# The last gated embedding and the final norm, turned so that tokens lie in the partitions

## What is computed

```python
def rmsnorm(x, g):
    y = x * lax.rsqrt(jnp.mean(x * x, axis=-1, keepdims=True) + 1e-6)
    return y * g

# end of the last layer (i = 1), h is [256, 1024], p[i] is [256, 256]
gate = jax.nn.sigmoid(rmsnorm(h, ple_norm[i]) @ ple_gate[i])   # ple_gate[i]: [1024, 1024]
h = h + (p[i] @ ple_proj[i]) * gate                            # ple_proj[i]: [256, 1024]
return rmsnorm(h, final_norm)
```

## Time and profile before

| | us |
|---|---|
| median of 3 runs (lowest, highest) | 1065.03 (1064.36, 1066.72) |
| the profiled execution's own time | 1066.18 |
| its span | 1064.4 |
| PE busy in the span | 1047.7 |
| DVE busy | 770.6 |
| ACT busy | 609.4 |
| first gate matmul of the last embedding starts | 1030.02 |
| its last gate matmul starts | 1054.12 |
| first of the four stores is issued | 1059.36 |

### The profile page before, as it was taken

How to read it: one execution, slowest core, us unless ns; L and a number is a source line. 1 busy time by engine, 2 the same in 40 slices (tenths; PEclk the granted TensorE clock), 3 DMA queues, 4 the chain that set the end, 5 groups by cost and what they waited for, 6 DMA issues and landing times.

```text
span 1064.4 us, 18866 instructions
## 1 busy us (share of the span) xinstructions
PE 1047.7 (98%) x7649; PEld 958.4 (90%) x7649; DVE 770.6 (72%) x943; ACT 609.4 (57%) x821; POOL 184.2 (17%) x196
## 2 busy tenths in 40 slices
PE   8999999999999999999999999999999999999997
PEld 8999999998898888888988888888999888888897
DVE  6778867889777667656887777566666777776566
ACT  6676655653266555544665555445677665655454
POOL 5999987300000000000000000000111000000000
PEclk9999999999999999999999999999999999999999
DMA  9765664531365656665556656666434556565562
GB/s 231 191 180 174 191 183 141 173 125 61 120 189 162 194 178 190 188 195 186 180 169 197 197 175 194 192 193 189 148 119 129 147 179 196 173 206 188 188 189 80
DMA packets 179679, 183.12 MB, mean 172 GB/s; under 512 B 16128, under 2 KB 173456, under 8 KB 179600
## 3 DMA queue, kind: packets, MB, share of 16 engines
q1 hardware_dynamic: 179456, 181.99, 56.9%
q10 hardware_dynamic: 144, 0.04, 0.0%
HBM read 180.95 MB, written 1.05 MB: 171 GB/s over the span
## 4 chain that ended last, share of the span: by engine, by line
PE 73%; DVE 10%; POOL 7%; issue 5%; ACT 3%; DMA 2%; POOLq 0%; SPq 0%; DVEq 0%; ACTq 0%
PE acc L2031 31%; PE acc L2033 16%; PE bank L1662 4%; PE bank L1663 4%; PE bank L1664 4%; POOL tmp L512 3%; DVE w_lo L1070 3%; PE acc L1662 3%; PE acc L1664 2%; PE acc L1663 2%; POOL dense L580 2%; ACT w_hi L662 2%; DMA raw<-in_ffn_w_dram 2%; POOL small L512 1%; PE stat L1789 1%
## 5 line engine op out<-in xcount | busy, mean ns | idle before, releaser
L1070 DVE TENSOR_TENSOR w_lo<-raw,w_hi 128x1024 fp32r<-128x1024 f32 x346 | 439.1, 1281 | 192.6 <-ACT w_hi L662 191.8
L662 ACT ACTIVATE w_hi<-raw 128x1024 fp32r<-128x1024 f32 x346 | 355.8, 1039 | 198.2 <-PE acc L2033 88.3
L2031 PE MATMUL acc<-op_both,w_hi 128*128 128x512 f32 x1056 | 368.8, 393 | 1.8 <-DVE w_lo L1070 0.9
L2033 PE MATMUL acc<-op_both,w_lo 128*128 128x256 f32 x1056 | 295.2, 280 | 0.0
L2031 PEld LDWEIGHTS acc<-op_both,w_hi 128*128 128x128 f32 x1056 | 198.2, 188 | 47.5 <-issue 3.8
L2033 PEld LDWEIGHTS acc<-op_both,w_lo 128*128 128x128 f32 x1056 | 198.3, 188 | 0.1
L2031 PE MATMUL acc<-g_all,w_hi 128*128 128x512 f32 x528 | 183.3, 392 | 0.2 <-issue 0.2
L1662 PE MATMUL bank<-op_both,w_hi 128*128 128x256 f32 x584 | 168.9, 289 | 2.2 <-DVE w_lo L1070 1.1
L1664 PE MATMUL bank<-op_both,w_hi 128*128 128x256 f32 x584 | 163.7, 280 | 0.0
L1663 PE MATMUL bank<-op_both,w_lo 128*128 128x256 f32 x584 | 163.7, 280 | 0.0
L2033 PE MATMUL acc<-g_all,w_lo 128*128 128x256 f32 x528 | 147.6, 280 | 0.0
(11 more groups left out here) (329 smaller groups left out, 1540.3 us busy)
## 6 DMA issues: line engine op xcount, KB each, us to landing
raw<-in_ffn_w_dram SPq DMA_DIRECT2D x258, 512.0 KB, 4.1
raw<-in_sb_w_qkv_dram SPq DMA_DIRECT2D x24, 512.0 KB, 3.6
raw<-in_s_w_glu_dram SPq DMA_DIRECT2D x16, 512.0 KB, 3.8
raw<-in_ple_gate_dram SPq DMA_DIRECT2D x16, 512.0 KB, 3.9
raw<-in_s_w_in_dram SPq DMA_DIRECT2D x8, 512.0 KB, 3.5
raw<-in_sb_w_o_dram SPq DMA_DIRECT2D x8, 512.0 KB, 3.5
raw<-in_ffn_w_dram SPq DMA_DIRECT2D x12, 256.0 KB, 3.2
raw<-in_ple_proj_dram SPq DMA_DIRECT2D x4, 512.0 KB, 3.7
```

The lines of the kernel that those rows point to most:

```text
L662: act.activation(w_hi[:, slot, 0:width], raw[:, slot, 0:width], ACT.Copy).then_inc(hi_done, 1)
L1070: dve.tensor_tensor(w_lo[:, slot, 0:width], raw[:, slot, 0:width], w_hi[:, slot, 0:width].bitcast(F32), ALU.subtract).then_inc(lo_done, 1)
L2031: pe.matmul(pairs[h][:, m].rearrange("p i t -> p (i t)"), wh, x.rearrange("p i t -> p (i t)"), start=first, stop=False, skip_group_check=True)
L2033: return pe.matmul(pairs[h][:, m, 0, :], wl, x[:, 0, :], start=False, stop=last, skip_group_check=True)
```

## The change

Only the last embedding and the final norm change (`ple_rows` on ACT, DVE and PE). The operand is now stationary and the weights move, so results have tokens in the partitions: two token blocks (`tb`) of 128 by two halves of 512 channels. The gate's chunks are 256 rows by 512 columns: four chunks for half 0, four for half 1. r is now one number for each partition, `r_col`, and goes in as the `scale` of ACT's sigmoid, so its spreading on PE (L1683), the copy to `r_row` and the product `a_n` go. `xT` is turned into rows by 16 transposes on PE between the gate's matmuls, and ACT copies them into `x_rows`. DVE multiplies by the projection, adds to `x_rows` and multiplies by the final gain, which is loaded once, spread over all partitions, into `gain_all` (one more transfer of SP, in the attention stage). The squares are summed along the free axis by ACT's accumulator (`accum_out`), so the sums on PE (L1676) go. DVE adds the parts up, POOL's power is done for each token block, and ACT and DVE scale and hand over to the stores. In half 1 the second token block is done in two parts of 256 columns, the second of them in a bank that half 0 of the first token block used before (`last_part_bank`).

```diff
+            def ple_rows(st):                                   # PE
+                def moving(o, xh, xl, wh, wl, start, stop):
+                    pe.matmul(o, xh, wh, start=start, stop=False, skip_group_check=True)
+                    pe.matmul(o, xh, wl, start=False, stop=False, skip_group_check=True)
+                    return pe.matmul(o, xl, wh, start=False, stop=stop, skip_group_check=True)
...
+                for i in range(4):
+                    pe.wait_ge(lo_done, n0 + 3 + i)
+                    for kk in range(2):
+                        pe.wait_ge(op_lo_done, KD * u + 2 * i + kk + 1)
+                        for tb in range(TB):
+                            mm = gate(tb, i, kk)
+                        if kk:
+                            mm.then_inc(pe_done, 1)
+                        if (i, kk) == (0, 1):
+                            turn_rows(0, 0)
+                        if (i, kk) == (1, 0):
+                            stat_sum(v)
+                        if (i, kk) == (2, 0):
+                            turn_rows(1, 0)
+                            turn_rows(0, 1)
+                        if (i, kk) == (3, 0):
+                            turn_rows(1, 1)
+                pe.wait_ge(x_rows_copied, 4)
+                for i in (4, 5):
+                    pe.wait_ge(lo_done, n0 + 3 + i)
+                    for kk in range(2):
+                        gate(0, i, kk)
+                    pe.wait_ge(gate_opened, 1)
+                    for kk in range(2):
+                        for part in parts:
+                            mm = gate(1, i, kk, part)
+                    mm.then_inc(pe_done, 1)
...
+            def ple_rows(st, nxt):                              # ACT
+                def open_gate(i, tb, half, part=slice(0, 512)):
...
+                    act.activation(gate_half[tb][:, part], g, ACT.Sigmoid,
+                                   scale=r_col[:, tb:tb + 1]).then_inc(gate_opened, 1)
...
+                split(n + 8)
+                open_gate(0, 0, 0)
+                open_gate(1, 1, 0)
+                split(n + 9)
...
+                act.wait_ge(rows_gained, 3)
...
+            def ple_rows(st, nxt):                              # DVE
...
+                weigh(3, 1, 1, slice(0, 256))
+                gain_rows_of(2, 0, slice(512, 1024))
+                part_mean(1, 0, 0, False)
+                part_mean(3, 0, 1, True)
+                weigh(4, 1, 1, slice(256, 512))
+                part_mean(3, 1, 0, False)
+                part_mean(4, 1, 1, False)
+                gain_rows_of(3, 1, slice(512, 768))
+                part_mean(5, 1, 2, True)
+                dve.wait_ge(r_ready, v + 1)
+                dve.wait_ge(rows_gained, 4)
+                scale_rows(0, 0)
...
+                sp.wait_ge(state_im, NB)                        # SP, attention stage
+                sp.dma_start(gain_all[:, :], final_norm.unsqueeze(0).broadcast_to([P, D])).then_inc(gain_all_landed, 16)
```

More of the change, by code:

```diff
@@ L247, in hybrid_trunk @@
         g_hi_done, g_lo_done = sem("g_hi_done"), sem("g_lo_done")
-        out_turned = sem("out_turned")
-        out_rows = [sem("out_rows0"), sem("out_rows1")]
+        rows_out = [[sem(f"rows_out{tb}{half}") for half in range(2)] for tb in range(2)]
         stored = sem("stored")
-        scaled = sem("scaled")
         def gain_col(st, k):
@@ L411, in load_group, with load_ple @@
                     load(n + half, (n + half) % RING, a_chunk(w, half, slice(col, col + 256)), True)
-            def load_ple(st):
+            def load_ple(st, nxt):
                 for kt in range(2):
                     load(st.n0 + kt, (st.n0 + kt) % RING, ple_proj[st.layer, kt * P:(kt + 1) * P, :], False)
+                if nxt.kind == "final":
+                    for i in range(8):
+                        half, kk, n = i // 4, i % 4, st.n0 + 2 + i
+                        src = ple_gate[st.layer, 256 * kk:256 * kk + 256, 512 * half:512 * half + 512]
+                        load(n, n % RING, src.rearrange("(k p) c -> p k c", p=P), True)
+                    return
                 for j in range(NB):
@@ L460, in _ @@
                         for half in range(2):
[L461 to L464, removed]
+                            cols = slice(half * 512, half * 512 + 512)
+                            sp.wait_ge(rows_out[tb][half], 1 + tb * half)
+                            sp.dma_start(out[0, tb * P:(tb + 1) * P, cols], x_rows[:, tb, cols]).then_inc(stored, 16)
                     sp.wait_ge(stored, 16 * 2 * TB)
@@ L800, in ple @@
                 split(st.n0 + 5)
-                groups = NB - 1 if nxt.kind == "final" else NB
-                for j in range(groups):
+                if nxt.kind == "final":
+                    ple_rows(st, nxt)
+                    return
+                for j in range(NB):
                     act.wait_ge(gate_taken, 4 * st.q + j + 1)
@@ L811, in ple @@
                         split(st.n0 + 12)
[L812 to L821, removed]
-                    act.activation(silu[:, m, :], a_n[:, m, :], ACT.Sigmoid).then_inc(gate_ready, 1)
-                act.wait_ge(squares_used, 4 * nxt.v + 2)
-                for m in range(2):
-                    act.wait_ge(x_new, 4 * nxt.v + j + m + 1)
-                    act.activation(squares[:, j % 2, m], xT[:, 2 * j + m, :], ACT.Square).then_inc(squared, 1)
+                    prep(nxt.v, nxt.u, [j])
@@ L1337, in ple @@
                 dve.wait_ge(r_row_ready, st.v + 1)
-                for j in range(NB - 1 if nxt.kind == "final" else NB):
+                for j in range(NB):
                     dve.wait_ge(pe_done, n0 + 4 + 2 * j)
```

249 lines of the change are left out of this document (153 added, 96 removed).

## The result

The changed kernel takes 1067.53 us (median of 20 runs, 1065.87 to 1068.92) against 1065.40 (20 runs, 1064.16 to 1066.72): 1.0020 times the time before, 95% interval 1.0014 to 1.0027, so 2.1 us slower. A second comparison on the chip, with 11 runs of it and 33 of the kernel before, gave 1.0013, interval 1.0004 to 1.0022, 1.4 us slower. The forecast was 1.4 us slower.

A forecast was written before the change was run, and what follows sets the result against it. PE, busy 98%, was taken to bound the kernel until the last gate matmul, then an unhidden chain. Terms: 2.92 - 1.56 = +1.36 us, taking the median from 1065.03 to 1066.4; 8-in-10 range 1064.3 to 1068.6.

The forecast's parts named there:

- A: First gate matmul to end of the last, on PE: 24.38 us before, forecast to grow by 2.92 us.
- wait of PE: Mid chunk 6, PE waits 1.86 us for ACT's first sigmoid, behind chunk 8's high part and the table load.
- changes between kinds of matmul: In half 0 on PE: 0.08 us for each of five changes, 0.1 for the first start, 0.50 in all.
- B: End of the last gate matmul to the first store's issue: 3.40 us instead of 4.96, 1.56 less.
- queue on DVE: In the tail, gain product and mean steps hold the last part's product behind its ready sigmoid, costing 0.5 us.
- the square with the reading of its accumulator: ACT's last square in the tail: 0.42 us, plus 0.23 for the accumulator's output.
- C: First store's issue to the end of the span, DMA engines full: stays at 5.04 us.
- the load: Final gain's extra 0.5 MB on SP in the attention stage: costs nothing, 1.3 us were the cover gone.
- rival 1: PE's clock falls behind the new sigmoid wait, decided by the wait's length: +1.4 us, 1067.8; chance 0.31.
- rival 2: ACT's table switch before the sigmoid also costs its drain: +1.38 us, 1067.8; chance 0.05.
- Rival 3: PE doesn't wait because the table loads while ACT waits for PE: median 1064.5; chance 0.09.
- rival 4: No PE wait, no DVE queue or accumulator cost in the tail, half the transposes hidden: 1062.9; chance 0.07.

The follow-up runs named there:

- table_early: Changed kernel with only the sigmoid's table load moved two high parts earlier on ACT, ahead of chunk 6's; 1065.18 us, ratio 0.9996 to the kernel before.
- no_wait: Changed kernel with table load ahead of chunk 6's high part, first sigmoid and DVE product ahead of chunk 8's split; 1063.86 us, 0.9989 of the kernel before.
- long_wait: Changed kernel with PE waiting for ACT's second sigmoid instead of its first in chunks 6 and 7; 1069.15 us, ratio 1.0037 to the kernel before.
- best: Changed kernel without PE's sigmoid wait, plus a reordered DVE tail and one store issued from ACT's queue; 1063.82 us, 0.9985 of the kernel before.
- few_turns: Changed kernel with 12 of the 16 transposes of xT left out, copies and waits kept; 1065.81 us, ratio 1.0003 to the kernel before.

## Why the prediction was right

**A.** Predicted +2.92, measured +2.68. The wait of PE was there, with the chain as told (high part 1.06, table 1.28, sigmoid 0.67 and no drain). The profile's 1.81 us count from the end of the last matmul, the 1.86 of the prediction from where the next one could have started; by the prediction's measure the wait was 1047.37 - 1045.16 - 0.233 = 1.98 us. 0.10 of the 0.12 more is that ACT's high part started 0.26 us behind the end of half 0 (1044.25 - 1043.99), not 0.16. table_early confirms the table's share and no_wait the whole. The term that was mis-sized is the changes between kinds of matmul, 0.50: half 0 took 13.46 us from 1030.53 to 1043.99, not 13.87. Four transposes with the slower start of the next matmul take 1034.08 - 1033.41 - 0.233 = 0.44 us, which is what 4 x 0.113 alone gives; I had added 0.08 for each change on top. The sum of squares did have its 0.08 on top, and the restart behind the wait cost 0.1, as assumed. The late start of ACT's chain gave back part of what this term had too much.

**B.** Predicted 3.40, measured 3.40, with two small errors that cancel. The queue on DVE cost 0.67 instead of 0.5 (the step at 1058.65 starts 0.11 us after the one ahead of it has ended), and the square with the reading of its accumulator took 0.51 us where I had 0.65, since they overlap. The power on one column takes 0.55 us, not 0.69, but it wasn't on the way to the first store. One step of the sum itself doesn't come out: 1055.15 and twice 0.69 are 1056.53, not 1056.62.

**C and the load.** 5.01 and nothing, as predicted.

**The clock, rival 1.** This was put as a fork: the clock falls behind the wait (0.31), or it doesn't. The runs show that it is no fork. It falls in some executions, in 2 of 8 profiles, and costs 1.5 us then, as priced (1.4). The step that failed is "it decides from a length of wait". The predicted 1066.4 is the kernel without falls in the stage (+1.36); there the stage grew by 0.9 to 1.1 us. The medians moved by 2.1 and 1.4 us, so that the forecast of 1.4 met the second of them so closely is in part luck.

Do falls behind the wait make up the difference? The record has the granted clock of the whole span of each timed run. Profiles with one fall ahead of the end have 0.995 to 0.998. 4 of the 20 runs of the first comparison have 0.994, and so do 3 of the 5 of long_wait, but none of the 61 runs of the kernel before in the two later comparisons, and none of the 11 of the second comparison. So some executions of the changed kernel very likely had a second fall; where it lay isn't seen. But without those four the median is 1067.4 still, 2.0 us above the kernel before, so they don't carry the 2.1 us. What does is open; the scatter ahead of the stage is as large.

**The other rivals.** The drain of the table load (rival 2) is absent: the sigmoid starts 0.02 us after the load ends. Rival 3 was excluded by the order of ACT's queue, as argued. Its own sum was too good, though: table_early is its mechanism, and PE still waits 0.39 us there, since the high part and the sigmoid still stand behind the end of half 0. The wait is gone only with the sigmoid ahead of the high part too, as in no_wait. Of rival 4, best has the tail with a shorter queue on DVE, and gets 1.5 of its 2.1 us below the kernel before; the half of the transposes that it wanted hidden was not, as few_turns shows. The chances give rivals 1 and 2 together 0.36, where the text has 0.35 for slower; that moves nothing.

## What to carry to other kernels

When a change puts an engine's result into the middle of another engine's dense work, follow the whole strict queue ahead of that result: here a table load that had been free stood behind a high part that waits for PE and cost 1.4 us, and one line moved it back under cover. Time an edit at the end of a long kernel by the stretch that it touches, since the medians carried over 1 us of scatter from code that was the same, and take more than one profile of either kernel. And a wait of PE near 2 us in dense work has to be priced twice, once as itself and once for the executions in which the clock falls behind it (here 1.5 to 1.6 us each); how large their share is has to be measured in the kernel at hand.

## What the runs showed of the hardware

- The clock of PE fell behind waits of 1.80 us in 8 of 16 pauses, behind 1.96 us in none of 16, behind 2.13 us in 2 of 16, and behind 1.50 and 1.67 us in none of 30, in one fixed order of pauses; each fall went to 0.50, the lower level, and cost 1.5 to 1.6 us.
- ACT's accumulator output comes as a separate instruction, ACTIVATION_READ_ACCUMULATOR, of 0.19 us, which starts 0.1 us before the row of the square has ended.
- POOL's power on 128 x 1 takes 0.55 us, on 128 x 2 0.69 before. The one in the last embedding takes 1.60 us in all twelve profiles with the new embedding and 0.69 in the two with the old. Beside it DVE now writes a low part (after: 1035.86 to 1037.08, the power from 1036.02), where before DVE waited; whether that is the cause wasn't tested. It cost nothing, since the first sigmoid comes 9 us later.
- When POOL sets single columns of 128 partitions one after the other, each adds 0.033 us, though the row of one shows 0.10 us.
